# Two transformer-like blocks on one core: three additions of squares move from GpSimd to VectorE, and one low half moves three steps

## Chip, core and metric

The kernel runs on one core of a Trainium2 chip. The metric is the device time of one execution in microseconds; below, the median of the runs.

## What is computed

The input x has 512 tokens of 1024 features. The first block is a Mamba-2 layer followed by a stick-breaking attention layer, the second a block with a gated recurrence, band attention and a feed-forward part. All is in float32. The change lies in the Mamba-2 layer, at the seam between its state space part and its output product:

```python
    y = y.reshape(b, s, M_D_INNER) * jax.nn.silu(z.astype(jnp.float32))
    yg = y.reshape(b, s, M_GROUPS, M_D_INNER // M_GROUPS)
    yg = yg * lax.rsqrt(jnp.mean(yg * yg, axis=-1, keepdims=True) + EPS)
    y = yg.reshape(b, s, M_D_INNER) * norm_g.astype(jnp.float32)
    return y.astype(h.dtype) @ out_w
```

The 2048 features of y are four groups of 512, which the kernel holds as four tiles Y[n] of 128 features by 512 tokens each. For each group it squares the four tiles, adds the four squares (three additions of 128x512), sums over the partitions with a matmul by ones, and takes the reciprocal root.

## The kernel before

Five engines run programs of their own, joined by semaphores. Each is in order. Every dense product in float32 is made of three matmuls in a reduced format: high half of the weights by high half of the input (L768), high by low (L769), low by high (L770). The weights stream in chunks of 1 MB into two raw buffers. ScalarE makes the high half of a chunk (L2240, whi), VectorE the low half, raw minus high (L1416, wlo), each in the call `behind(kind, n)` that names the block after whose chunk the next one comes. `behind("out", 2)` thus makes the halves for output blocks 4 and 5. SyncE loads the chunk after next into a raw buffer when the low half is made that read it.

The state space part, `ssd()` on each engine, is a generator over units u = -1 to 18, four steps each; unit u is chunk u mod 4 (128 tokens) of group u div 4. `group_step(u, later)` says which group is due: with `GROUP_UNITS` = {4: 1, 8: 2, 13: 3, 16: 4} the third group (`y2`, tiles Y[8] to Y[11]) has its gate in unit 13, its squares in units 13 and 14, its sum in unit 15 and its normalisation in unit 16.

Units 12 to 18 run beside `out_pair()`, the output blocks 0 to 7 of 8 steps each. `weave((out_pair(), 66), (chunks, 28))` hands out the steps of the two generators in proportion 66 to 28, at build time, on TensorE, VectorE and ScalarE alike; on GpSimd the units run alone. Out of it come these orders around the change (worked out from the step counts):

- VectorE: ..., ST mul 13, ST add 13, gate of group 3 (L1627, four tiles), residuals 0 and 1 (L1689), read_y(13) (L1558, then four of L1563 on XS), E times CB of unit 14 (L1598), low half behind out 2 (L1416), YT 14 (L1605), XD 15 (L1577), ST mul 14 (L1613), ST add 14 (L1616), residual 2, read_y(14), E times CB 15, YT 15, residual 3, low half behind out 4, read_y(15), residual 4, gate of group 4, normalisation of group 3 (L1636), ...
- TensorE: ..., out 3 step 0, y 14 (L923), out 3 steps 1 to 3, state times Cc of unit 15 (L891, waits for ST add 14), out 3 steps 4 to 7, out 4 step 0, sum of group 3 (L792, waits for the three additions), out 4 steps 1 and 2, y 15, out 4 steps 3 to 7, out 5, ...
- ScalarE: ..., squares 1 and 2 of group 3 (L2274), high half behind out 2, exponentials of unit 15 (L2421, L2424, which wait for a load of AC), square 3, EA 15 (L2437, L2438), square 4, high half behind out 4, reciprocal root of group 3 (L2261, L2262, with a table load before it), ...
- GpSimd: the three additions (L2922), and nothing else in this stage.

The squares and additions take turns in two buffers, SQ and R: squares 1 and 2 go to SQ and R, addition 0 makes SQ += R, square 3 is written to R after it, addition 1, square 4 into R, addition 2. The semaphore s_sq counts squares and s_sqa additions.

Of the kernel before, what the change touches and what calls it, by code (L numbers as in the profile page):

```python
# [10 lines left out]
ALU = mybir.AluOpType  # L11
# [205 lines left out]
def program(nc, wstream, astream, tstream, crow, vec, con, masks, xT, pT, rbx, out, scratch, pscr):  # L217
# [1128 lines left out]
    def _(e):  # L1346
# [204 lines left out]
        def read_y(p):  # L1551
# [15 lines left out]
            else:  # L1567
                own(x)

        def scaled_inputs(u):  # L1570

            gv, cv_ = divmod(u + 1, 4)
            hs, xd = slice(8 * gv, 8 * gv + 8), xd_at(u + 1)
            w.wait_ge(s_tx, u + 2)
            if slot_free(u + 1):
                w.wait_ge(s_yd, slot_free(u + 1))
            e.tensor_tensor(xd[:, :, :], heads(aux[0]), dtk[:, cv_, hs].unsqueeze(2).to_broadcast([128, 8, 64]),  # L1577
                            ALU.mult).then_inc(s_xd, 1)
            if cv_ < 3:
                w.wait_ge(s_wex, 1)  # L1580
                w.wait_ge(s_xd, u + 2)
                w.wait_ge(s_ts, 3 * gv + cv_)
                e.tensor_tensor(XW[:, :, :], xd[:, :, :], WE[:, cv_, hs].unsqueeze(2).to_broadcast([128, 8, 64]),
                                ALU.mult).then_inc(s_xw, 1)

        def ssd():
            for u in range(-1, 19):
                g, c = divmod(u, 4)
                for p in Y_READ.get(u, ()):
                    read_y(p)  # L1590
                if 0 <= u < 16:
                    if c == 0:
                        w.wait_ge(s_cbp, g + 1)
                        e.tensor_tensor(CB[:, :, :], quads(aux[1]), cmask.unsqueeze(1).to_broadcast([128, 4, 128]),
                                        ALU.mult).then_inc(s_cb, 1)
                    w.wait_ge(s_cb, g + 1)
                    w.wait_ge(s_ee, u + 1)
                    e.tensor_tensor(e_at(u), e_at(u), CB[:, c, :].unsqueeze(1).to_broadcast([128, 8, 128]),  # L1598
                                    ALU.mult).then_inc(s_m, 1)
                yield  # L1600
                if 0 <= u < 16:
                    if c > 0:
                        w.wait_ge(s_to, 3 * g + c)
                        w.wait_ge(s_ea, 3 * g + c)
                        e.tensor_tensor(yt_at(u), quads(aux[3]), EA[:, :, :], ALU.mult).then_inc(s_tyo, 1)  # L1605
                    if u in (12, 13, 14):
                        scaled_inputs(u)
                    if c == 0:
                        w.wait_ge(s_ts, 3 * g + 1)
                        w.wait_ge(s_to, 3 * g)  # L1610
                        e.tensor_copy(ST[:, :, :], heads(aux[4][:, :])).then_inc(s_st, 1)
                    elif c < 3:
                        own(e.tensor_tensor(ST[:, :, :], ST[:, :, :],  # L1613
                                            EL[:, c, 8 * g:8 * g + 8].unsqueeze(2).to_broadcast([128, 8, 64]), ALU.mult))
                        w.wait_ge(s_ts, 3 * g + c + 1)
                        e.tensor_tensor(ST[:, :, :], ST[:, :, :], heads(aux[4][:, :]), ALU.add).then_inc(s_st, 1)  # L1616
                yield
                if u < 12:
                    scaled_inputs(u)
                if u in (1, 5, 9):  # L1620
                    read_y(u - 1)
                y = group_step(u, 0)
                if y > 0:
                    w.wait_ge(s_fin, 10 * y)
                    for q in range(4):
                        n = 4 * (y - 1) + q
                        e.scalar_tensor_tensor(Y[:, n, :], XS[(y - 1) % 2][:, q, :], 0.5, Y[:, n, :],  # L1627
                                               ALU.mult, ALU.mult).then_inc(s_y, 1)
                yield
                y = group_step(u, 3)  # L1630
                if 0 < y < 4:
                    w.wait_ge(s_rr, SUM_AT[f"y{y - 1}"])
                    w.wait_ge(s_y, 4 * y)
                    o = VOFF["m_norm_g"][0]
                    for n in range(4 * y - 4, 4 * y):
                        e.scalar_tensor_tensor(Y[:, n, :], Y[:, n, :], cv[:, o + n:o + n + 1], R,  # L1636
                                               ALU.mult, ALU.mult).then_inc(s_yn, 1)
                yield

        first, chunks = in_proj(0), ssd()  # L1640
# [52 lines left out]
        def out_pair():  # L1693
            gated(39)
            yield
            for n in range(8):
                for step in range(8):
                    if n == 0 and step < 4:
                        low("out0", 4 + step, Y[:, 4 + step, :])
                    if step == 4 and n % 2 == 0:  # L1700
                        behind("out", n)
                    if step == 6 and n in (5, 6):
                        ada_dot(11 + n)
                    if n == 7 and step > 3:
                        low("out2", step - 4, Y[:, 4 + step, :])
                    if step == 7 and n > 0:
                        if n == 1:
                            residual("out", 0, 0, 16)
                        residual("out", n, n, 16)
                    yield  # L1710
            ada_dot(18)
# [1202 lines left out]
    @blk.gpsimd  # L2914
    def _(e):
        w = Once(e)

        def add(sq, n, tile, acc=SQ):

            w.wait_ge(s_sq, sq)  # L2920
            w.wait_ge(s_sqa, n - 1)
            e.tensor_tensor(acc, acc, tile, ALU.add).then_inc(s_sqa, 1)  # L2922

        def add_x(name, k):
            if k > 0:
                add(SQ_AT[name] + k + 1, SA_AT[name] + k, T[(k - 1) % 3][:, :])

        def in_proj(g):
            for hb in range(10 * g, 10 * g + 10):
                yield from idle(8)  # L2930

        def ssd():
            for u in range(-1, 19):
                g, c = divmod(u, 4)
                for n in range(4):
                    y = group_step(u, 1)
                    if y > 0 and n % 2 == 0:
                        add(SQ_AT[f"y{y - 1}"] + 2 + n // 2, SA_AT[f"y{y - 1}"] + 1 + n // 2, R)
                    y = group_step(u, 2)
                    if y > 0 and n == 0:  # L2940
                        add(SQ_AT[f"y{y - 1}"] + 4, SA_AT[f"y{y - 1}"] + 3, R)
                    yield

        def out_proj(g):
            yield
            for n in range(8):
                yield from idle(3)
                if g == 3:
                    add_x("out", n)
                yield  # L2950

        chunks = ssd()
        run(take(chunks, 4))
        for g in range(1, 4):
            weave((in_proj(g), 80), (take(chunks, 16), 16))
        run(chunks)
        run(chain(out_proj(2), out_proj(3)))

        w.wait_ge(s_av, 8)
        e.memset(AD[:, :, :, :], 0.0).then_inc(s_zero, 1)  # L2960
        e.memset(OFF[0][:, :, :], 0.0).then_inc(s_zero, 1)
        for n in range(1, 8):
            for m, acc in ((2 * n - 2, R), (2 * n - 1, SQ)):
                add(SQ_AT["so"] + m + 3, SA_AT["so"] + m + 1, T[m % 3][:, :], acc)

        def load_bias(n):
            if n < 4:
                w.wait_ge(l_bw[n % 2], 128 + 16 * (n // 2 + 1))
                e.memset(BW[n % 2][0:64, :, 448:512], -1e30).then_inc(s_bw, 1)

        def band():
            for r in range(-1, 19):
                if r % 4 == 0 or r < 0:
                    load_bias((r + 4) // 4)
                yield from idle(3)

        def gates_a():
            for n in range(8):
                yield from idle(8)

        def branch_a():
            for n in range(8):
                yield from idle(4)

        dense_a = chain(gates_a(), branch_a())
        run(take(dense_a, 5))
        weave((band(), 60), (dense_a, 87))
        for n in range(8):
            add_x("wo", n)
        for i11 in range(11):  # L2990
            n = 2 * i11 + 1
            w.wait_ge(s_fh, n + 1)
            e.tensor_tensor(FL[:, n, :], T[n % 3][:, :], FH[:, n, :].bitcast(F32), ALU.subtract).then_inc(s_fl2["G"], 1)
        for i4 in range(4):
            add_x("fd", 2 * i4)
            add_x("fd", 2 * i4 + 1)
# [69 lines left out]
```

## Time and profile before

| | |
|---|---|
| median of 3 runs | 1488.93 us (1488.75 to 1489.31) |
| profiled execution | 1489.0 us, its span 1487.1 us |
| TensorE, weight load | 1479.1 us (99%), 1191.8 us (80%) |
| VectorE | 959.2 us (65%) |
| ScalarE | 674.5 us (45%) |
| GpSimd | 99.2 us (7%) |
| granted TensorE clock | full in all slices |

Times in the rows are microseconds from the span's start. The durations of matmuls are modelled and overlap, so their starts are read, not their lengths. An instruction's duration on VectorE overlaps the next one's by some 0.08 us; the distance from start to start is what it takes of the queue.

### The profile page before, as it was taken

To read this page: it belongs to the slowest core of one execution; us is meant where nothing else is said; L and a number is where in the kernel's file an instruction comes from. 1 tells how busy PE (TensorE), PEld (TensorE's weight loads), DVE (VectorE), ACT (ScalarE), POOL (GpSimd) and SP (SyncE) were. 2 spreads that over 40 slices of the span, in tenths; PEclk is the share of its full clock that TensorE was granted. 3 is DMA by queue.
4 is the path that set the end of the run, shared out by engine and by line. 5 is a ranking of instruction groups with operands and counts; after the bars stand their busy time and mean duration, and the time that the engine had idled before them with its cause. 6 is when DMAs were issued, how large, how long until landed. Compare 5 with 4: busy or idle time off the path is not lost.

```text
span 1487.1 us, 19779 instructions
## 1 busy us (share of the span) xinstructions
PE 1479.1 (99%) x8054; PEld 1191.8 (80%) x8054; DVE 959.2 (65%) x1232; ACT 674.5 (45%) x968; POOL 99.2 (7%) x68
## 2 busy tenths in 40 slices
PE   9999999999999999999999999999999999999998
PEld 5788888878888877778888877788888888888887
DVE  5869899998896788845468367745544434432445
ACT  4656566764452567754223445423332222322232
POOL 0000001011300000024000000000300000000210
PEclk9999999999999999999999999999999999999999
DMA  9344354434586322223212342132222322232223
GB/s 395 122 152 160 114 171 142 156 105 151 205 315 216 114 85 71 73 85 115 86 61 84 115 143 85 58 106 93 95 104 85 112 87 95 104 106 78 100 100 127
DMA packets 49314, 184.60 MB, mean 124 GB/s; under 512 B 4116, under 2 KB 21012, under 8 KB 33096
## 3 DMA queue, kind: packets, MB, share of 16 engines
q1 hardware_dynamic: 32400, 174.76, 32.9%
q10 hardware_dynamic: 16824, 8.58, 2.4%
q8 instruction: 64, 1.05, 0.3%
q14 instruction: 26, 0.21, 0.0%
HBM read 174.83 MB, written 4.30 MB: 120 GB/s over the span
## 4 chain that ended last, share of the span: by engine, by line
PE 97%; DVE 2%; issue 1%; DMA 0%; ACT 0%; DVEq 0%; ACTq 0%
PE bank L768 26%; PE bank L770 26%; PE bank L769 26%; PE bank L1111 1%; PE tt L1088 1%; PE bank L1028 1%; PE bank L1030 1%; PE bank L1029 1%; PE tt L923 1%; PE zz L1257 1%; PE zz L1100 1%; PE zz L1099 1%; PE bank L1270 1%; PE tt L891 1%; PE zz L1191 1%; PE tt L1244 1%
## 5 line engine op out<-in xcount | busy, mean ns | idle before, releaser
L768 PE MATMUL bank<-HH,whi 128*128 128x512 f32 x1336 | 538.0, 403 | 0.4 <-DVE HL L1368 0.3
L770 PE MATMUL bank<-HH,wlo 128*128 128x512 f32 x1336 | 521.5, 390 | 0.0
L769 PE MATMUL bank<-HL,whi 128*128 128x512 f32 x1336 | 520.7, 390 | 0.0
L1416 DVE TENSOR_TENSOR wlo<-raw,whi 128x2048 fp32r<-128x2048 f32 (+1 forms) x129 | 262.9, 2040 | 97.9 <-ACT whi L2240 91.1
L768 PEld LDWEIGHTS bank<-HH,whi 128*128 128x128 f32 x1336 | 251.0, 188 | 62.4 <-issue 11.9
L770 PEld LDWEIGHTS bank<-HH,wlo 128*128 128x128 f32 x1336 | 250.7, 188 | 53.6
L769 PEld LDWEIGHTS bank<-HL,whi 128*128 128x128 f32 x1336 | 251.3, 188 | 49.7 <-issue 2.6
L2240 ACT ACTIVATE whi<-raw 128x2048 fp32r<-128x2048 f32 (+1 forms) x107 | 202.3, 1891 | 137.5 <-PE bank L770 111.1
L2922 POOL TENSOR_TENSOR SRT<-SRT 128x512 f32<-128x512 f32 x47 | 81.7, 1737 | 644.8 <-ACT SRT L2274 643.1
L770 PE MATMUL bank<-FH,wlo 128*128 128x512 f32 x176 | 68.5, 389 | 0.0
L769 PE MATMUL bank<-FL,whi 128*128 128x512 f32 x176 | 68.5, 389 | 0.0
L768 PE MATMUL bank<-FH,whi 128*128 128x512 f32 x176 | 68.5, 389 | 0.0
L2171 DVE TENSOR_TENSOR pst<-bank,SRT 128x512 f32<-128x512 f32 x22 | 15.1, 692 | 72.0 <-PE bank L770 72.0
L2183 DVE SCALAR_TENSOR_TENSOR SRT<-SRT,bank 128x512 f32<-128x512 f32 x22 | 15.1, 688 | 65.0 <-PE bank L770 65.0
L1849 DVE TENSOR_TENSOR_SCAN keeps<-keeps,cc 128x511 f32<-128x511 f32 (+3 forms) x64 | 49.0, 808 | 6.3 <-ACT TW L2640 6.2
L2891 ACT ACTIVATE FH<-SRT 128x512 fp32r<-128x512 f32 x22 | 13.9, 633 | 85.8 <-DVE SRT L2183 85.8
L2887 ACT ACTIVATE SRT<-pst 128x512 f32<-128x512 f32 x22 | 13.9, 632 | 82.4 <-DVE pst L2171 82.4
L2274 ACT ACTIVATE SRT<-X 128x512 f32<-128x512 f32 x32 | 20.1, 629 | 67.9 <-DVE X L1682 53.2
L768 PEld LDWEIGHTS bank<-FH,whi 128*128 128x128 f32 x176 | 33.0, 188 | 7.0
L770 PEld LDWEIGHTS bank<-FH,wlo 128*128 128x128 f32 x176 | 33.0, 188 | 6.9
L769 PEld LDWEIGHTS bank<-FL,whi 128*128 128x128 f32 x176 | 33.0, 188 | 6.7
L768 PE MATMUL bank<-WH,whi 128*128 128x512 f32 x96 | 38.2, 398 | 0.0
(380 smaller groups left out, 2131.4 us busy)
## 6 DMA issues: line engine op xcount, KB each, us to landing
raw<-wstream SPq DMA_DIRECT2D x113, 1024.0 KB, 4.8
aslot<-tstream SPq DMA_DIRECT2D x24, 512.0 KB, 3.7
AD<-tstream SPq DMA_DIRECT2D x24, 512.0 KB, 5.4
A<-astream SPq DMA_DIRECT2D x8, 1024.0 KB, 17.8
AC<-scratch ACTq DMA_DIRECT2D x16, 512.0 KB, 5.2
QD<-QD SPq DMA_DIRECT2D x16, 256.0 KB, 4.0
raw<-wstream SPq DMA_DIRECT2D x4, 768.0 KB, 4.1
X<-xT SPq DMA_DIRECT2D x2, 1024.0 KB, 6.7
```

Source lines behind the costliest of these rows:

```text
L768: e.matmul(o, wh[:, k, c], hi[:, kb0 + k, :], start=first and k == 0, stop=False)
L769: e.matmul(o, wh[:, k, c], lo[:, kb0 + k, :], start=False, stop=False)
L770: x = e.matmul(o, wl[:, k, c], hi[:, kb0 + k, :], start=False, stop=last and k == kb - 1)
L891: x = e.matmul(aux[3][:, 128 * q:128 * q + 128], flat(ST[:, 2 * q:2 * q + 2, :]), Cc[g % 2][:, 128 * c:128 * c + 128], start=True, stop=True)
L923: x = e.matmul(y_bank(v)[o:o + 64, 128 * q:128 * q + 128], xd_at(v)[:, h, :], e_at(v)[:, h, :], start=True, stop=True)
L1416: x = e.tensor_tensor(wlo[:, i % 2, c], raw[:, i % 2, c], whi[:, i % 2, c].bitcast(F32), ALU.subtract)
L1849: x = e.tensor_tensor_scan(k, k, diag[:, last], 0.0, ALU.mult, ALU.add)
L2171: e.tensor_tensor(pstage[n % 3][:, :], bank_of("fg", n)[:, :], R, ALU.mult).then_inc(s_fgr, 1)
L2183: e.scalar_tensor_tensor(q, q, 0.5, bank_of("fu", n)[:, :], ALU.mult, ALU.mult).then_inc(s_fu, 1)
L2240: e.activation(whi[:, i % 2, 0:n], raw[:, i % 2, 0:n], ACT.Copy).then_inc(s_hi, 1)
L2274: e.activation(dst, src, ACT.Square, scale=scale).then_inc(s_sq, 1)
L2922: e.tensor_tensor(acc, acc, tile, ALU.add).then_inc(s_sqa, 1)
```

## The change

Group 3's three additions leave GpSimd's program and stand in VectorE's, each with its two waits, for the square that it adds and for the addition before it. The low half behind out 2 is made at step 7 of output block 2, where it stood at step 4.

```diff
+        def add_square(n):
+
+            w.wait_ge(s_sq, SQ_AT["y2"] + 2 + n)
+            w.wait_ge(s_sqa, SA_AT["y2"] + n)
+            e.tensor_tensor(SQ[:, :], SQ[:, :], R, ALU.add).then_inc(s_sqa, 1)
...
+                if group_step(u, 1) == 3:
+                    add_square(0)
+                if group_step(u, 2) == 3:
+                    add_square(2)
                 yield
                 if u < 12:
                     scaled_inputs(u)
...
+                if group_step(u, 1) == 3:
+                    add_square(1)
                 yield
...
-                    if step == 4 and n % 2 == 0:
+                    if step == (7 if n == 2 else 4) and n % 2 == 0:
                         behind("out", n)
...
-                    if y > 0 and n % 2 == 0:
+                    if y > 0 and y != 3 and n % 2 == 0:
                         add(SQ_AT[f"y{y - 1}"] + 2 + n // 2, SA_AT[f"y{y - 1}"] + 1 + n // 2, R)
                     y = group_step(u, 2)
-                    if y > 0 and n == 0:
+                    if y > 0 and y != 3 and n == 0:
                         add(SQ_AT[f"y{y - 1}"] + 4, SA_AT[f"y{y - 1}"] + 3, R)
```

VectorE's order after it: ..., read_y(13), E times CB 14, YT 14, XD 15, ST mul 14, ST add 14, addition 0, low half behind out 2, residual 2, addition 1, read_y(14), E times CB 15, YT 15, addition 2, residual 3, low half behind out 4, ... TensorE's, ScalarE's and SyncE's programs are not touched, nor are the other three groups' additions.

## Rows read from the trace of the kernel before

**Rows 1.** The page, busy time and instructions of each engine.

```profile
PE 1479.1 (99%) x8054; PEld 1191.8 (80%) x8054; DVE 959.2 (65%) x1232; ACT 674.5 (45%) x968; POOL 99.2 (7%) x68
```

**Rows 2.** TensorE's waits: us in total, times, longest.

```profile
PE zz L834 <- DVE HL L1434: 1.6, 1, 1.6
...
PE tt L891 <- DVE ST L1616: 0.2, 1, 0.2
```

**Rows 3.** Windows: length, busy us of PE, PEld, DVE, ACT, POOL; clock, DMA share, GB/s.

```profile
0.00:20.00 20.00, 16.92 (x74) 8.80 (x75) 8.47 (x33) 9.79 (x20) 0.21 (x4) 1.00 0.91 370
...
320.00:330.00 10.00, 9.76 (x54) 7.21 (x52) 9.85 (x15) 6.85 (x9) 2.58 (x2) 1.00 0.32 105
330.00:1450.00 1120.00, 1119.81 (x6132) 908.26 (x6129) 658.45 (x785) 457.71 (x602) 85.75 (x55) 1.00 0.32 111
1450.00:1487.10 37.10, 32.91 (x168) 28.04 (x166) 20.51 (x29) 8.88 (x11) 0.00 (x0) 1.00 0.36 128
```

**Rows 4.** Timeline of TensorE: start, us, instruction, idle before and releaser in brackets.

```profile
322.38 0.39 PE L770 MATMUL bank<-HH,wlo 128*128 128x512 f32 x1
323.01 1.16 PE L891 MATMUL tt<-Cc,ST 128*128 128x128 f32 x8 [0.24 <-DVE ST L1616]
...
326.77 0.39 PE L768 MATMUL bank<-HH,whi 128*128 128x512 f32 x1
...
327.23 0.39 PE L770 MATMUL bank<-HH,wlo 128*128 128x512 f32 x1
327.46 1.02 PE L792 MATMUL zz<-SRT,cc 128*128 128x512 f32 x2
```

**Rows 5.** Timeline of VectorE, 315 to 335 us.

```profile
315.64 1.33 DVE L1563 SCALAR_TENSOR_TENSOR XS<-XS,cv,YT 128x128 f32<-128x128 f32 x4
317.01 1.23 DVE L1598 TENSOR_TENSOR E<-E,CB 128x1024 f32<-128x1024 f32 x1
318.15 2.29 DVE L1416 TENSOR_TENSOR wlo<-raw,whi 128x2048 fp32r<-128x2048 f32 x1
320.35 0.68 DVE L1605 TENSOR_TENSOR YT<-tt,EA 128x512 f32<-128x512 f32 x1
...
321.55 0.68 DVE L1613 TENSOR_TENSOR ST<-ST,EL 128x512 f32<-128x512 f32 x1
322.26 0.69 DVE L1616 TENSOR_TENSOR ST<-ST,bank 128x512 f32<-128x512 f32 x1
322.87 0.74 DVE L1689 SCALAR_TENSOR_TENSOR X<-bank,ada,X 128x512 f32<-128x512 f32 x1
323.53 0.68 DVE L1558 TENSOR_TENSOR YT<-tt,YT 128x512 f32<-128x512 f32 x1
324.25 2.24 DVE L1563 SCALAR_TENSOR_TENSOR XS<-XS,cv,YT 128x128 f32<-128x128 f32 x4
326.52 1.23 DVE L1598 TENSOR_TENSOR E<-E,CB 128x1024 f32<-128x1024 f32 x1
327.67 0.68 DVE L1605 TENSOR_TENSOR YT<-tt,EA 128x512 f32<-128x512 f32 x1
...
331.98 1.14 DVE L1563 SCALAR_TENSOR_TENSOR XS<-XS,cv,YT 128x128 f32<-128x128 f32 x4
334.73 0.75 DVE L1689 SCALAR_TENSOR_TENSOR X<-bank,ada,X 128x512 f32<-128x512 f32 x1 [1.61 <-PE bank L770]
```

**Rows 6.** Timeline of GpSimd: the first and the third addition of group 3.

```profile
314.73 1.30 POOL L2922 TENSOR_TENSOR SRT<-SRT 128x512 f32<-128x512 f32 x1 [55.65 <-ACT SRT L2274]
...
324.26 1.30 POOL L2922 TENSOR_TENSOR SRT<-SRT 128x512 f32<-128x512 f32 x1 [0.74 <-ACT SRT L2274]
```

**Rows 7.** Timeline of ScalarE: exponentials of unit 15, squares 3 and 4, table load.

```profile
318.09 2.45 ACT L2421 ACTIVATE E<-AC,atk 128x128 f32<-128x128 f32 x8 [1.62 <-DMA AC<-scratch]
...
321.54 0.62 ACT L2274 ACTIVATE SRT<-Y 128x512 f32<-128x512 f32 x1
...
323.55 0.63 ACT L2274 ACTIVATE SRT<-Y 128x512 f32<-128x512 f32 x1 [0.23 <-POOL SRT L2922]
...
328.97 1.28 ACT L2265 ACT_TABLE_LOAD   x1
```

## Prediction

> **What bounds the kernel now.** I read the page's busy line first: TensorE is busy 1479.1 of 1487.1 us, VectorE 959.2 [rows 1]. Then the list of TensorE's waits, where the reader is to see how little is left: 1.6 us at the start and, in the whole stage that the change touches, one wait of 0.2 us for ST [rows 2]. The windows say the same: 3.08 us of the 8.0 us that TensorE is idle lie in the first 20 us, 4.19 us in the last 37 us, and 0.19 us in the 1120 us between this stage and those [rows 3]. So TensorE's order is the kernel's time, nothing behind this stage can swallow a delay, and a microsecond lost or won in front of a matmul here is one of the kernel's. The change can win only the wait for ST, and can lose whatever it puts in its place.
>
> TensorE's timeline has that wait and the next dependence on VectorE's side [rows 4]. The matmuls of L891 (state times Cc for unit 15) start at 323.01, where the pace of 0.23 us from one matmul to the next (327.23 to 327.46) would have put them at 322.61: it costs 0.40 us, of which 0.24 us shows as idle. The sum of squares of the third group (L792) starts at 327.46 and waits for nothing. It needs all three additions.
>
> VectorE's timeline is the view that decides [rows 5]: it works without a gap from 315.6 to 333.1 us, where it first waits (1.61 us, until 334.73). It is the full engine here, so what stands ahead of an instruction in its queue sets that instruction's time. GpSimd is nearly empty: its third addition starts at 324.26 and ends at 325.56, 1.9 us before the sum [rows 6]. ScalarE's third square starts at 321.54 and its fourth at 323.55, released by the second addition [rows 7].
>
> **The low half moves back.** Now it takes 318.15 to 320.35, a step of 2.20 us, ahead of YT 14, XD 15, and the two ST instructions on whose end TensorE waits [rows 5]. Moved behind them, it lets the last ST instruction end 2.2 us earlier: the 0.40 us is won. Its own user is the first matmul of output block 4, at 326.77 [rows 4], or 326.37 after the gain; below it comes out ready at 323.4, so 3 us of cover. SyncE's load into that raw buffer waits for it and is issued about 3 us later, but the block that it serves comes two chunks on. ScalarE's high half of the same chunk comes from the buffer read, not from the low half. These are priced at nothing; with the cover gone, each microsecond would be one.
>
> **The additions leave GpSimd.** What goes is 3 times 1.3 us on an idle engine, worth nothing in itself. But VectorE's four XS instructions beside the third addition took 2.24 us, and 1.33 us beside the first, against 1.14 us with GpSimd idle [rows 5, 6]. That gives VectorE 1.10 + 0.19 = 1.29 us back; the most that could be charged to GpSimd is the whole overlap, 1.30 us of the third addition and 316.03 - 315.64 = 0.39 us of the first, 1.69 us, which I keep as an end of the range. The page "SBUF — State Buffer" of the Trainium skill (section "Who interferes with whom") says that a VectorE instruction with two SBUF inputs and a GpSimd instruction that reads SBUF exclude each other for the whole instruction. By that rule the whole overlap would come back and the stall below would be 0.4 us shorter; the rows say 1.29 us, and the sum goes by them.
>
> **The additions on VectorE.** No row shows this form there. Nearest are additions of the same shape: 0.69 us busy, 0.60 us from start to start (two in 1.20 us from 320.35 to 321.55), 0.71 us where the next one depends on it (321.55 to 322.26) [rows 5]. I take 0.61 us in the queue (322.26 to 322.87) and 0.69 us until it counts; the ends are 0.60 and 0.72.
>
> What matters more is where they land. By the weave, add_square(0) stands behind the second ST instruction of unit 14, add_square(1) behind the residual of block 2, and add_square(2) behind read_y(14), E times CB of unit 15 and YT 15. On GpSimd the third waited only for its square. On VectorE it waits for all of those.
>
> **The queue worked out**, from start to start, all from [rows 5]: E times CB of unit 14 at 317.01 - 0.19 = 316.82; plus 1.14, YT 14 at 317.96; plus 1.20 for it and XD 15, first ST at 319.16; plus 0.71, second ST at 319.87; plus 0.61, add_square(0) at 320.48, done 321.17; plus 0.61, low half at 321.09, done 323.38; plus 2.20, residual 2 at 323.29; plus 0.66, add_square(1) at 323.95, done 324.64; plus 0.61, YT of read_y at 324.56; plus 0.72, XS at 325.28; plus 2.27 - 1.10, E times CB of unit 15 at 326.45; plus 1.15, YT 15 at 327.60; plus 0.61, add_square(2) at 328.21, done 328.90.
>
> Do the squares come in time? ScalarE reaches the third at 321.54 as before, since add_square(0) is done at 321.17; add_square(1) wants it only at 323.95 and it is done at 322.16. The fourth starts once add_square(1) is done, 324.64 + 0.04, done 325.3, 2.9 us before add_square(2) [rows 7]. The new waits hold up nothing in VectorE's queue.
>
> **The sum.** From the end of the last ST instruction (322.26 + 0.69) to TensorE's start it took 0.06 us [rows 4, 5]. The sum of squares thus starts at 328.96. It stood at 327.46, and without a wait would now stand at 327.06: TensorE loses 1.90 us and has won 0.40 us, net +1.50 us. Everything behind it moves along. YT 15 no longer waits; the residual of block 4 waits for TensorE already (1.61 us idle before it at 334.73 [rows 5]), so the fourth group's chain hangs on TensorE and shifts as it does. The reciprocal root's table load starts at 328.97 now, 1.5 us after the sum [rows 7]; the normalisation that reads its result comes behind that residual, 5 us after, so there is no second loss. The granted clock is 1.00 (2.4 GHz) in the first 20 us, with their 3.08 us of gaps, and in this stage [rows 3], so I price no fall of it.
>
> Against the profiled execution: 1489.0 + 1.5 = 1490.5 us. The median of the runs is 1488.93, 0.07 us under it, so 1490.4 us. The ends: with the whole overlap given back (0.40 us more), +1.1; with additions of 0.72 us (+0.33) and a restart of TensorE that costs 0.1 us more, +1.95. That is 1490.0 to 1490.9.
>
> **Rivals.** (1) The sum isn't held up, and only the wait for ST goes: 1489.0 - 0.4 - 0.1 = 1488.5 us. For it: the change does remove that wait with 2.2 us to spare. Against it: add_square(2) would have to be done at 327.0, 1.9 us earlier than worked out, which is more than three whole additions in a queue without a gap. It could come true in part if VectorE's instructions run closer than in the profile. (2) Slower, by the chain squares-additions-squares that now blocks VectorE. The third square stands on ScalarE behind the exponentials of unit 15, and those waited 1.62 us for the load of AC until 318.09 [rows 7]. If that load lands later by d, the third square is done at 322.16 + d, and add_square(1) stops VectorE's whole queue, with read_y(14), E times CB 15, YT 15 and the last addition behind it. It decides from d = 323.95 - 322.16 = 1.8 us, and each microsecond beyond is one for TensorE. With d = 3.5 us the time is 1490.4 + 1.7 = 1492.1 us. Against it: nothing that the change moves delays this load; the raw load that could meet it, now after 320.5, moves away from it. (3) Nothing that can be seen: gain and loss cancel, with add_square(2) done near 327.5; about 1489.0. It needs 1.4 us that the rows don't have.
>
> **How the numbers follow.** A difference under 0.2% (3.0 us) is about what a measurement of this kernel can't tell from no change. The forecast has 0.80 (net +1.1 to +1.95, within 0.2%), rivals 1 and 3 together 0.11 (within 0.2%), rival 2 0.06 (slower). The other 0.03 is for what I don't see, 0.02 on the faster side and 0.01 on the slower. So faster 0.02, within 0.91, slower 0.07. The range goes from rival 1, 1488.4, to the upper end of the forecast and the 0.3 us by which runs differ, 1491.2; the forecast's own is 1490.0 to 1490.9.
>
> **What would show it.** In the changed profile: no wait at L891 of unit 15; a wait of 1.6 to 2.0 us at L792 near 327 us, released by VectorE's addition, and that addition ending near 328.9; XS of read_y(14) at 1.14 us, not 2.24; the last square released by the second addition near 324.7. If L792 doesn't wait, the queue sum is wrong and rival 1 holds. If add_square(1) shows idle time before it, released by a square, rival 2 has begun. If the span grows by more than the wait at L792, something behind it was not tied to TensorE.

## Result and the profile after

| | before | after |
|---|---|---|
| median of 22 runs each | 1488.82 us | 1490.83 us (1490.15 to 1492.24) |
| ratio, 95% interval | | 1.0016 (1.0010 to 1.0022) |
| forecast | | 1490.4 us, range 1488.4 to 1491.2 |
| profiled execution, its span | 1489.0, 1487.1 us | 1492.06, 1490.3 us |

By the medians the change costs 2.0 us, 0.14%; by the means it is 1.0016, the table's ratio. The median is only half of it: the 22 runs are two clusters with nothing between them. Twelve lie from 1490.15 to 1490.92 (median 1490.57, +1.75 us), ten from 1491.75 to 1492.24 (median 1492.01, +3.19 us). In the ten the mean granted clock over the run is 0.999, in the twelve 1.000. (By itself that mean is no sign of a fall here: of 33 runs of the kernel before beside the first experiments, eight have 0.999 too, and in its profile the clock falls only behind the last matmul.) The profiled execution is one of the ten.

The page's busy line, against [rows 1]:

```profile
PE 1480.3 (99%) x8054; PEld 1192.7 (80%) x8054; DVE 960.0 (64%) x1235; ACT 674.9 (45%) x968; POOL 95.4 (6%) x65
```

VectorE has three instructions more and GpSimd three fewer; nothing else moved in number. TensorE's waits (us in total, times, longest), against [rows 2], where L792 doesn't appear:

```profile
PE zz L792 <- DVE SRT L1574: 1.9, 1, 1.9
PE zz L834 <- DVE HL L1434: 1.6, 1, 1.6
```

The wait of L891 for ST is gone and L792, the sum of squares, waits 1.9 us for the third addition (L1574 is the new line). VectorE's timeline shows why, against [rows 5] (start, us, instruction):

```profile
316.61 1.22 DVE L1604 TENSOR_TENSOR E<-E,CB 128x1024 f32<-128x1024 f32 x1
...
319.67 0.69 DVE L1622 TENSOR_TENSOR ST<-ST,bank 128x512 f32<-128x512 f32 x1
320.27 0.68 DVE L1574 TENSOR_TENSOR SRT<-SRT 128x512 f32<-128x512 f32 x1
320.87 2.29 DVE L1416 TENSOR_TENSOR wlo<-raw,whi 128x2048 fp32r<-128x2048 f32 x1
323.07 0.75 DVE L1701 SCALAR_TENSOR_TENSOR X<-bank,ada,X 128x512 f32<-128x512 f32 x1
323.73 0.68 DVE L1574 TENSOR_TENSOR SRT<-SRT 128x512 f32<-128x512 f32 x1
324.33 0.69 DVE L1558 TENSOR_TENSOR YT<-tt,YT 128x512 f32<-128x512 f32 x1
325.06 1.14 DVE L1563 SCALAR_TENSOR_TENSOR XS<-XS,cv,YT 128x128 f32<-128x128 f32 x4
326.23 1.23 DVE L1604 TENSOR_TENSOR E<-E,CB 128x1024 f32<-128x1024 f32 x1
327.37 0.68 DVE L1611 TENSOR_TENSOR YT<-tt,EA 128x512 f32<-128x512 f32 x1
327.97 0.68 DVE L1574 TENSOR_TENSOR SRT<-SRT 128x512 f32<-128x512 f32 x1
```

The additions take 0.68 us each and 0.60 us of the queue, XS has 1.14 us again, and the third addition ends at 328.65 (327.97 + 0.68). TensorE's timeline around it, against [rows 4]:

```profile
326.48 0.39 PE L770 MATMUL bank<-HH,wlo 128*128 128x512 f32 x1
328.80 1.93 PE L792 MATMUL zz<-SRT,cc 128*128 128x512 f32 x2 [1.93 <-DVE SRT L1574]
329.74 1.42 PE L768 MATMUL bank<-HH,whi 128*128 128x512 f32 x1
330.96 0.63 PE L769 MATMUL bank<-HL,whi 128*128 128x512 f32 x1
331.38 0.63 PE L770 MATMUL bank<-HH,wlo 128*128 128x512 f32 x1
...
332.83 1.09 PE L923 MATMUL tt<-E,XD 128*64 128x128 f32 x16
```

Two things are to be seen: the gap of 1.93 us, and behind it matmuls that start 0.42 us apart where they started 0.23 us apart. The windows of TensorE show what that is (start and end, length, busy us, granted clock, DMA share, GB/s), against [rows 3]:

```profile
326.00:327.00 1.00, 0.87 (x4) 1.00 0.95 401
327.00:328.00 1.00, 0.00 (x0) 1.00 0.38 156
328.00:329.00 1.00, 0.20 (x1) 0.96 0.00 0
329.00:330.00 1.00, 1.00 (x3) 0.50 0.00 0
330.00:331.00 1.00, 1.00 (x3) 0.50 0.00 0
331.00:332.00 1.00, 1.00 (x4) 0.50 0.00 0
332.00:333.00 1.00, 1.00 (x7) 0.83 0.44 74
333.00:334.00 1.00, 1.00 (x17) 1.00 0.80 303
```

The granted clock falls from 1.00 (2.4 GHz) to 0.50 (1.2 GHz) at about 328.9, some 0.1 us after the sum has started, and is back at about 332.3. So the gap itself still shows the full clock (1.00 from 327 to 328, 0.96 from 328 to 329), and it is the matmuls behind it that run slowly. ScalarE's fourth square is released by the second addition, as forecast, against [rows 7]:

```profile
324.45 0.63 ACT L2286 ACTIVATE SRT<-Y 128x512 f32<-128x512 f32 x1 [1.61 <-DVE SRT L1574]
```

and GpSimd has nothing to do until the fourth group, against [rows 6]:

```profile
344.86 1.30 POOL L2934 TENSOR_TENSOR SRT<-SRT 128x512 f32<-128x512 f32 x1 [85.97 <-ACT SRT L2286]
```

### The profile page after: what moved, and what is told of

It reads as the page before. It is cut to its first block, busy times and chain, and to the rows that moved or that the text cites. A ratio compares the mean times of both kernels' runs of the same rounds, so it can differ in the third digit from the quotient of the medians.

```text
span 1490.3 us, 19779 instructions
## 1 busy us (share of the span) xinstructions
PE 1480.3 (99%) x8054; PEld 1192.7 (80%) x8054; DVE 960.0 (64%) x1235; ACT 674.9 (45%) x968; POOL 95.4 (6%) x65
## 4 chain that ended last, share of the span: by engine, by line
PE 96%; DVE 2%; issue 1%; DMA 0%; ACT 0%; DVEq 0%; ACTq 0%
PE bank L768 26%; PE bank L770 26%; PE bank L769 25%; PE bank L1111 1%; PE tt L1088 1%; PE bank L1028 1%; PE bank L1029 1%; PE bank L1030 1%; PE tt L923 1%; PE zz L1257 1%; PE zz L1100 1%; PE zz L1099 1%; PE bank L1270 1%; PE zz L1191 1%; PE zz L792 1%
## 5 line engine op out<-in xcount | busy, mean ns | idle before, releaser
L2934 POOL TENSOR_TENSOR SRT<-SRT 128x512 f32<-128x512 f32 x44 | 77.7, 1767 | 651.8 <-ACT SRT L2286 650.1
```

## Experiments

The theory after the result: the third addition stands too late in VectorE's queue, TensorE stands idle ahead of the sum, and in part of the executions its clock falls for it, in the gap or just behind. The rivals: the moved low half costs something; VectorE's added 1.8 us of work cost something wherever they stand; the upper cluster has nothing to do with the gap. Twelve experiments ran (the changed kernel and the filled one stand among them again), each 11 times unless said otherwise, in three groups, each group on one chip beside the kernel before. A difference is against the median of the kernel before in its group; these were 1488.94 (first four), 1488.89 (next four) and 1488.54 us (last four). The ranges behind a ratio are its 95% interval. Each gap below is read from the one profiled execution of its kernel; whether the clock fell in the other executions is inferred from the cluster in which their times lie.

### One part of the change alone

The low half alone:

```diff
-                    if step == 4 and n % 2 == 0:
+                    if step == (7 if n == 2 else 4) and n % 2 == 0:
                         behind("out", n)
```

> The kernel before with the low half behind out 2 at step 7 alone; the additions stay on GpSimd. Theory (the loss is TensorE's gap ahead of the sum of squares, and the clock that falls in it): no gap at L792, no wait at L891 of unit 15, so 0.3 to 0.5 us under the kernel before, 1488.4 us, and no run with a lower clock. Rival (the moved low half is late for a user and costs part of the 2 us): 1489.3 us or more, with a new wait at output block 4 or behind it.

Measured: 1488.48 us, 0.46 us under the kernel before (ratio 0.9997, 0.9989 to 1.0006). TensorE waits neither at L891 nor at L792 nor at a user of the low half. The step is harmless, and the difference has the size that was worked out, though the interval holds no change too.

The additions alone (the changed kernel, with that line back):

> The changed kernel with the low half back at step 4: only the additions are moved. Theory: the third addition still ends near 328.7 us, since the low half stands ahead of it in either place; L891 waits again for up to 0.2 us and the gap at L792 is about 1.8 us. The time is that of the changed kernel, 1490.6 us where the clock holds and about 1492.0 where it falls. Rival (the two edits hurt each other, the additions alone are harmless): 1489.0 us.

Measured: 1490.70 us, +1.76 us (1.0012, 1.0003 to 1.0020), all 11 runs from 1490.40 to 1491.02. The gap is a little shorter, and no run is in the upper cluster:

```profile
328.85 1.10 PE L792 MATMUL zz<-SRT,cc 128*128 128x512 f32 x2 [1.74 <-DVE SRT L1574]
331.27 1.09 PE L923 MATMUL tt<-E,XD 128*64 128x128 f32 x16
```

Here the clock held: from L792 to L923 it takes 2.42 us, in the changed profile 4.03 us, so the low clock costs 1.61 us in that execution. The expected runs near 1492.0 didn't come; the additions alone explain the lower cluster. The upper one came with the gap 0.2 us longer, which is what the low half's move adds by making TensorE early (L891 starts at 322.54 here and at 322.40 in the changed profile); 11 runs of one kernel can't show alone that those 0.2 us decide.

### The same additions without the gap

The sum one step later on TensorE, behind the y matmuls of unit 15:

```diff
-                if 0 < y < 4:
+                if 0 < y < 3:
                     w.wait_ge(s_cb, y + 1)
                     sum_of(f"y{y - 1}", aux[1], n=3)
                 yield
...
                     x.then_inc(s_cbp, 1)
+                if group_step(u, 2) == 3:
+                    sum_of("y2", aux[1], n=3)
```

> The changed kernel with the matmul that sums group 3 one step later on TensorE, behind the y matmuls of unit 15, where the third addition should be done. Theory: no wait at L792, none at L891, time 0.3 to 0.5 us under the kernel before, 1488.4 us. Rival (moving the additions slows VectorE or its users elsewhere): 1489.0 or more.

Measured: 1488.27 us, 0.67 us under the kernel before (0.9996, 0.9987 to 1.0005), all runs within 1488.12 to 1488.37. TensorE meets no wait:

```profile
328.23 1.09 PE L923 MATMUL tt<-E,XD 128*64 128x128 f32 x16
329.25 1.12 PE L792 MATMUL zz<-SRT,cc 128*128 128x512 f32 x2
```

All three additions are on VectorE, their last ends at 328.7, and it costs nothing once TensorE has other work until then. This has the lowest median of all kernels here; by its interval it can't be called faster than the kernel before.

The third addition earlier in VectorE's queue (here behind read_y(14)):

```diff
                     read_y(p)
+                if group_step(u, 2) == 3:
+                    add_square(2)
...
-                if group_step(u, 2) == 3:
-                    add_square(2)
```

> The changed kernel with the third addition two places further up VectorE's queue, behind read_y(14) and ahead of E times CB of unit 15. By the changed profile it would start at 326.2 us and end at 326.9, where TensorE reaches the sum at 326.9. Theory: gap of 0 to 0.2 us, no fall of the clock, 1488.5 us. Rival (the cost isn't the place of the addition but that VectorE makes it at all, 1.8 us of its time): 1490 us.

Measured: 1488.79 us beside 1488.89 (0.9999, 0.9990 to 1.0008); 0.20 us of gap is left at L792. It is 0.3 us above what was expected, about what is left of the gap.

### The place as a dose

Ahead of YT 15, 0.6 us earlier than in the change:

> The changed kernel with the third addition one place further up, ahead of YT 15 and behind E times CB of unit 15: 0.6 us earlier, so a gap of 1.3 us at L792 instead of 1.93. Theory: 1490.0 us where the clock holds; whether a gap of 1.3 us still lets it fall is open, and if it does less often than in 10 of 22 runs the length of the gap counts. Rival (not this gap): 1490.6 us and as many runs near 1492.0 as in the changed kernel.

Measured: gap 1.34 us, 1489.96 us (all runs from 1489.47 to 1490.17; ratio 1.0007, 0.9998 to 1.0016), no run above. The median is where it was expected, though the interval holds no change too, and none of 11 runs shows a fall at this gap.

Behind residual 3, 0.66 us later:

> The changed kernel with the third addition behind residual 3, 0.66 us later: a gap of 2.6 us at L792 by the changed profile. Theory: 1491.2 us where the clock holds and 1.4 us more, 1492.7, where it falls, and it falls in a larger share of the runs than in the changed kernel. Rival (the share doesn't grow with the gap): the same share.

Measured (9 runs): median 1492.31 us (1.0023, 1.0013 to 1.0032); four runs from 1490.55 to 1491.23, five from 1492.31 to 1492.88. The profiled execution is one of the four: behind a gap of 2.59 us its clock stays at 1.00. Five of nine is more than 14 of 33 (below), but with so few runs the growth isn't shown.

Behind the low half behind out 4, 2.9 us later:

> The changed kernel with the third addition behind residual 3 and the low half behind out 4: 0.66 + 2.20 = 2.9 us later than in the changed kernel, a gap of 4.8 us. Theory: 1490.6 + 2.9 = 1493.5 us with the clock held; if the clock falls for about as long as in the changed profile, 1.4 us more, 1494.9 us, and now in all runs: one cluster. Rival (the gap is covered by something behind it): less than 1493.

Measured (5 runs): 1495.42 us (all runs from 1494.55 to 1496.18; ratio 1.0044, 1.0031 to 1.0057). No run near 1493.5. The sum's row in the timeline:

```profile
332.01 2.04 PE L792 MATMUL zz<-SRT,cc 128*128 128x512 f32 x2 [4.79 <-DVE SRT L1574]
```

The clock in the gap and behind it, in the windows' columns as above:

```profile
330.00:331.00 1.00, 0.00 (x0) 0.83 0.00 0
331.00:332.00 1.00, 0.00 (x0) 0.50 0.00 0
332.00:333.00 1.00, 0.99 (x2) 0.50 0.76 131
333.00:334.00 1.00, 1.00 (x3) 0.50 0.81 344
334.00:335.00 1.00, 1.00 (x4) 0.50 0.95 401
335.00:336.00 1.00, 1.00 (x4) 0.50 0.42 172
336.00:337.00 1.00, 1.00 (x6) 0.50 0.00 0
337.00:338.00 1.00, 1.00 (x16) 0.76 0.00 0
```

Here the clock is down at about 330.7, before TensorE resumes, and stays down until about 337.5, longer than in the changed profile. That is 5.5 us of work at half the clock, by estimate 2.7 us lost, and 1493.5 + 2.7 = 1496.2 us is what this execution took (1496.18). It is the slowest of the five; that the others lie lower because their clocks were down for less of the work, and with them the median at 0.5 us above the expected 1494.9, is likely but not shown.

### The gap without the additions

The kernel before, with one wait more on TensorE:

```diff
                     w.wait_ge(s_cb, y + 1)
+                    if y == 3:
+                        w.wait_ge(s_res, res_at["out", 3])
                     sum_of(f"y{y - 1}", aux[1], n=3)
```

> The kernel before, additions on GpSimd and the low half where it was, but TensorE's sum of group 3 also waits for residual 3 on VectorE, which ends at 329.0 us by the trace of before: a gap of 1.6 us and nothing else changed. Theory: 1488.8 + 1.6 = 1490.4 us where the clock holds, and 1.4 us more in the runs where it falls. Rival (moving the additions itself costs time): 1489.0 us.

Measured: 1490.69 us, +1.80 us (1.0011, 1.0003 to 1.0020), all runs from 1489.97 to 1491.21 in one cluster.

```profile
329.11 1.10 PE L792 MATMUL zz<-SRT,cc 128*128 128x512 f32 x2 [1.41 <-issue]
```

Residual 3 ends on VectorE at 329.00 in this profile, just ahead of the sum. (The profile names no releaser; the one wait added is that one.) The sum starts 1.65 us later than in [rows 4] and the kernel is about that much longer, with not one addition moved. So the loss is the late sum, not the additions as such. The idle column says 1.41 us and not 1.6: the last matmul's modelled end overlaps the time at which the next would have started, 0.23 us after it.

### The clock: the gap with work in it

Two matmuls of constants by ones ahead of the sum, into the bank that the sum overwrites; nothing else changed:

```diff
                     w.wait_ge(s_cb, y + 1)
+                    if y == 3:
+                        for _ in range(2):
+                            e.matmul(aux[1][:, :], ones, diag, start=True, stop=True)
                     sum_of(f"y{y - 1}", aux[1], n=3)
```

> The changed kernel with two more 128x512 matmuls of constants by ones in front of the sum of group 3, into the bank that the sum then overwrites; each takes 0.86 us, so they fill 1.7 of the 1.93 us in which TensorE waits, and nothing waits for them. Theory that the clock falls because TensorE stands idle there: all runs at full clock, in one cluster near 1490.6 us, none near 1492.0. Rival (the two clusters, 1490.2 to 1490.9 and 1491.8 to 1492.2, have another cause, such as the data load or where the run happens to be placed): still four or five runs in ten near 1492.0.

Measured: 1490.30 us (ratio 1.0009, 1.0000 to 1.0018), all 11 runs from 1489.98 to 1490.73. To be sure that the chip wasn't the reason, the changed kernel and the filled one ran once more side by side, with one that has a single filling matmul:

> The changed kernel once more, unaltered, on the same chip as the next three. Theory (a gap of 1.9 us lets the clock fall in part of the executions): again two clusters, some four in ten runs near 1492.0 us and the rest near 1490.6. Rival (the upper cluster belonged to the chips or the moment of those runs): one cluster near 1490.6.

> The kernel with two matmuls of constants in the gap once more, beside the changed kernel on one chip. Theory: one cluster at 1490.3 us, with none above 1491.3, whatever the changed kernel does here. Rival (the fall is not tied to TensorE standing idle): as many upper runs as the changed kernel has here.

> The changed kernel with one matmul of constants (0.86 us) at the start of the gap, which leaves about 1.0 us of it. Theory: the clock holds as it did with a gap of 1.3 us, one cluster at 1490.4 us. Rival: some runs near 1492.0.

Measured: the changed kernel again in two clusters (median 1490.39 us), seven runs from 1490.04 to 1490.73 and four from 1491.56 to 1492.00; filled, 1490.30 us, all within 1489.91 to 1490.45; half filled (0.98 us of gap left), 1490.53 us, all within 1490.21 to 1491.28. The profiles of the filled and of the changed kernel of that group:

```profile
326.58 1.88 PE L914 MATMUL zz<-cc 128*128 128x512 f32 x4
328.58 1.13 PE L792 MATMUL zz<-SRT,cc 128*128 128x512 f32 x2
```

```profile
328.66 1.10 PE L792 MATMUL zz<-SRT,cc 128*128 128x512 f32 x2 [1.92 <-DVE SRT L1574]
332.15 1.56 PE L923 MATMUL tt<-E,XD 128*64 128x128 f32 x16
```

This execution of the changed kernel (1491.72 us) is one of the upper cluster too, and its clock falls later than in the first profile, at about 329.7, when TensorE has been at work again for 1.1 us:

```profile
328.00:329.00 1.00, 0.34 (x1) 1.00 0.00 0
329.00:330.00 1.00, 1.00 (x4) 0.87 0.00 0
330.00:331.00 1.00, 1.00 (x4) 0.50 0.00 0
```

The sum starts at the same time in both, since it waits for the same addition. Useless work in the gap doesn't shorten the wait, but it takes away the upper cluster: 0 of 22 filled runs, 14 of 33 of the changed kernel. That settles that the fall comes of TensorE standing idle there. It is worth 1.44 us between the medians of the first measurement's clusters.

| gap at L792, us | 0.98 | 1.34 | 1.41 | 1.74 | 1.93 | 2.59 | 4.79 |
|---|---|---|---|---|---|---|---|
| runs in the upper cluster | 0 of 11 | 0 of 11 | 0 of 11 | 0 of 11 | 14 of 33 | 5 of 9 | 5 of 5 |

## Why the prediction was right and wrong

**Right: what bounds, and the new wait.** TensorE's order is the time; the wait for ST went, the wait at L792 came, released by VectorE's third addition, with nothing behind to swallow it. The new wait at this place was the core of the forecast, and the additions-alone and wait-alone kernels bear it out, with +1.76 and +1.80 us. The forecast's range for it, 1490.0 to 1490.9, holds all 12 runs of the lower cluster but one (1490.92).

**Right: the queue sum.** Of the steps worked out from [rows 5], the ST addition was put at 319.87 and came at 319.67, the low half at 321.09 and 320.87, the third addition at 328.21 and 327.97. All lie 0.2 us early because this execution starts VectorE's stage that much earlier; the distances hold within 0.05 us. From start to start the four XS instructions gave back 1.10 us beside the third addition and 0.19 us beside the first, as the sum had it. The most that the prediction allowed for after the Trainium skill's page "SBUF — State Buffer" (section "Who interferes with whom"), the whole overlap and so 0.4 us more, didn't come.

**A little off: the net of the gap, 1.5 us.** L792 moved from 327.46 to 328.80, and the stage starts 0.21 us earlier in this execution (316.61 for E times CB, where 316.82 was worked out): 1.55 us net, as forecast. What the working left to the upper end is the restart: from L792 to L923 it takes 2.34 us before (327.46 to 329.80) and 2.42 us behind a gap with the clock held. That makes 1.63 us; the runs of the lower cluster say 1.75, and where the last 0.1 us comes from isn't shown. It is inside the forecast's own range, 1.1 to 1.95.

**Wrong: the step that priced no fall of the clock.** I took the first 20 us, with 3.08 us of gaps and the clock at 1.00 [rows 3], as the nearest rows. But a sum of gaps isn't one gap: of TensorE's waits the longest is 1.6 us [rows 2], and that one lies ahead of its first matmul; the next longest in that list is 0.9 us. The new one is 1.93 us, and no gap inside the kernel showed what the clock does then. The stretch behind the last matmul did, and I hadn't looked at it. In the trace of before that matmul ends at 1482.91, the clock stays at 1.00 for some 3.9 us more and falls at about 1486.8:

```profile
1480.00:1483.00 3.00, 2.91 (x25) 1.00 0.23 87
1483.00:1484.00 1.00, 0.00 (x0) 1.00 0.00 0
...
1486.00:1487.00 1.00, 0.00 (x0) 0.91 0.22 76
```

That is a fall on idleness in a kernel with a full clock everywhere else, and it isn't the same from one execution to the next: in the 13 profiles taken of the other kernels it comes from 1.95 us (the filled kernel) to 4.9 us (the low half alone) behind the last matmul. So the fall should have been a rival with a price and a chance. The term that stood at nothing measured 1.44 us in 14 of 33 executions, moved the median from 1490.57 to 1490.83 and the upper runs to 1492.24, a microsecond beyond the range. That the median still lies inside the range is luck: it is the top of the lower cluster, and with one run more in the upper one (11 and 11) it would have been about 1491.3. The Trainium skill's page "TensorE: Matmul & The Clock Gate" (section "HAM oscillation — how this bites in real kernels") says that waits for data can send the engine back to its low clock, so that work after each wait starts cold; the waits in its example are longer than this one, and this trace shows the same behind a gap of 1.93 us, with 0.50. I had not weighed it.

**Wrong: what the measurement can tell.** I called a difference under 0.2% (3.0 us) about what a measurement can't tell from no change, and so put 0.91 on "within 0.2%" and 0.07 on slower. The ratio lies within 0.2%, but with 22 runs a side the interval ends at 1.0010: the change is slower beyond its interval. The number forecast was +1.5 us; calling it unmeasurable was the error. No row gave the 3.0 us: the three runs on record lay within 0.56 us of each other, and the 22 of the kernel before lie within 0.6 us of their median. The additions-alone kernel stands out of the noise with no fall of the clock: +1.76 us in 11 runs, with an interval from 1.0003.

**Rivals.** (1) no hold-up at L792: false, 1.93 us. (Its time, 1488.5 us, is also 0.1 us off the 1488.4 from which the range starts.) (2) a late load of AC that blocks VectorE at the second addition: no idle time stands ahead of it in the profile, which is an execution of the upper cluster, and the filled kernel, with the same chain, has no upper runs. (3) cancelling: false.

## What to carry to other kernels

An addition moved from an idle engine to a full one in order doesn't cost its own duration but its place: here 1.8 us of work cost nothing when TensorE's use of it stood one step later, and 1.75 us when it didn't. Before moving work, write down the time at which its reader comes and everything queued ahead of it on the new engine. Where a change opens a gap on TensorE longer than any in the trace, price the clock as a case of its own, see what it does behind the kernel's last matmul, and look at single runs: two clusters are hidden by a median.

## What was not expected of the hardware

One wait of 1.9 us on TensorE, in a kernel whose matmul engine is 99% busy, was enough to drop the granted clock to 0.50, from about 328.9 to 332.3 us in the first profiled execution, which cost 1.61 us there and 1.44 us between cluster medians. Both profiled executions of the changed kernel show the fall, and by their times 14 of 33 had it. With gaps of 0.98 to 1.74 us it happened in none of 44, with 4.79 us in all 5. The fall can come after the wait is over: 0.1 and 1.1 us behind the start of the sum in the two profiles. Why the same gap does it in one execution and not in the next is open; the fall behind the last matmul, at 1.95 to 4.9 us, varies as well. Matmuls of constants that filled the gap kept the clock up at no cost (1490.30 us, where the changed kernel's lower runs in the same group have 1490.26), since the engine had to wait there anyway.
